# Splitting the modulation products of both first-block layers over three places of a one-core Trainium2 kernel

## The reference, cut to what matters

```python
def adaln(cond, w_mod, b_mod):
    return jnp.split(jax.nn.silu(cond) @ w_mod + b_mod, 6, axis=-1)      # w_mod: 1024 x 6144

for i in range(DEPTH):                                                   # 2 layers
    sh1, sc1, gt1, sh2, sc2, gt2 = adaln(c, w_mod[i], b_mod[i])
    csh1, csc1, cgt1, csh2, csc2, cgt2 = adaln(c_ctx[None, :], w_mod[i], b_mod[i])
    x, ctx = mixer_sublayer(x, ctx, (sh1, sc1, gt1), (csh1, csc1, cgt1), lp, rope, update_ctx)
    x = x + gt2[:, None, :] * peer_ffn(modulate(rmsnorm(x, g_norm2[i]), sh2, sc2), ...)
    if update_ctx:
        ctx = ctx + cgt2[:, None, :] * peer_ffn(modulate(rmsnorm(ctx, g_norm2[i]), csh2, csc2), ...)
```

## Time and profile before

| | us |
|---|---|
| median of 3 runs | 4714.18 (4707.75 to 4722.7) |
| profiled execution, time | 4724.5 |
| profiled execution, span | 4722.7 |
| mean granted TensorE clock | 0.867 of full |
| TensorE matmul busy | 3695.1 (78%) |
| VectorE busy | 2504.9 (53%) |
| moved by DMA | 1093.51 MB, 232 GB/s over the span |

### The profile page before, as it was taken

How to read it: one execution, slowest core, us unless ns; L and a number is a source line. 1 busy time by engine, 2 the same in 40 slices (tenths; PEclk the granted TensorE clock), 3 DMA queues, 4 the chain that set the end, 5 groups by cost and what they waited for, 6 DMA issues and landing times. The chain is left out here.

```text
span 4722.7 us, 46191 instructions
## 1 busy us (share of the span) xinstructions
PE 3695.1 (78%) x15562; PEld 2891.4 (61%) x15562; DVE 2504.9 (53%) x4840; ACT 627.5 (13%) x1654; POOL 1355.6 (29%) x1156
## 2 busy tenths in 40 slices
PE   5677989469988999967982444445999898998898
PEld 2345878458777777745771111113886787886787
DVE  0236557798788676654548878664433201333300
ACT  1223011230000000012210000101011201001200
POOL 0026000005665566623104777773000000000000
PEclk7787999699999999977896677767997799998799
DMA  9401844339999999950645999998861344771242
GB/s 338 155 13 40 243 123 119 103 117 406 409 409 377 409 409 409 409 196 30 181 154 218 386 372 363 390 394 299 277 209 45 107 134 143 243 245 50 90 151 98
DMA packets 549997, 1093.51 MB, mean 232 GB/s; under 512 B 29572, under 2 KB 315268, under 8 KB 549030
## 3 DMA queue, kind: packets, MB, share of 16 engines
q1 hardware_dynamic: 398216, 549.92, 34.0%
q0 software_dynamic: 147456, 536.94, 29.3%
q10 hardware_dynamic: 4128, 4.19, 0.3%
HBM read 1074.16 MB, written 16.78 MB: 231 GB/s over the span
## 5 line engine op out<-in xcount | busy, mean ns | idle before, releaser
L1897 PE MATMUL ps<-gv,diag 128*128 128x512 f32 x512 | 302.8, 757 | 402.3 <-DMA gv<-in_v_tab,eid 292.0
L1633 POOL DMA_INDIRECT gu<-in_u_tab,eid x256 | 346.2, 1353 | 837.4 <-DVE gate L1280 493.4
L2342 PE MATMUL ps<-hT,wring 128*128 128x256 f32 x2560 | 559.3, 379 | 0.2 <-DMA wring<-in_ffn_w_up 0.2
L1598 PE MATMUL ps<-hT,wring 128*128 128x256 f32 x2048 | 483.1, 390 | 76.9 <-DVE hT L1753 75.1
L2342 PEld LDWEIGHTS ps<-hT,wring 128*128 128x128 f32 x2560 | 486.2, 190 | 66.9 <-DVE hff L2409 0.6
L1598 PEld LDWEIGHTS ps<-hT,wring 128*128 128x128 f32 x2048 | 388.2, 193 | 166.3 <-DVE hT L1753 115.1
L1897 PEld LDWEIGHTS ps<-gv,diag 128*128 128x128 f32 x512 | 123.2, 248 | 580.2 <-issue 463.7
L1591 PE MATMUL ps<-hT,wring 128*128 128x256 f32 x2048 | 463.5, 379 | 1.4 <-ACT G L1674 1.4
L1591 PEld LDWEIGHTS ps<-hT,wring 128*128 128x128 f32 x2048 | 389.6, 190 | 54.5 <-issue 1.6
L2003 DVE CUSTOM_DVE_ANT_0 junk<-gu,htok 128x1024 f32<-128x1024 f32 x256 | 313.7, 1225 | 141.3 <-DMA gu<-in_u_tab,eid 133.3
L1777 DVE SCALAR_TENSOR_TENSOR wring<-gv,wgt,wring 128x1024 f32<-128x1024 f32 x254 | 326.4, 1285 | 112.2 <-DMA gv<-in_v_tab,eid 107.4
(11 more groups left out here) (317 smaller groups left out, 4721.3 us busy)
## 6 DMA issues: line engine op xcount, KB each, us to landing
wring<-in_u_first SPq DMA_DIRECT2D x128, 512.0 KB, 9.2
wring<-in_v_tab SPq DMA_DIRECT2D x128, 512.0 KB, 6.8
wring<-in_w_mod SPq DMA_DIRECT2D x24, 2048.0 KB, 12.9
lslot<-in_ada_w SPq DMA_DIRECT2D x32, 1536.0 KB, 10.5
wring<-in_ffn_w_gate SPq DMA_DIRECT2D x44, 1024.0 KB, 8.8
wring<-in_ffn_w_up SPq DMA_DIRECT2D x44, 1024.0 KB, 11.2
wring<-in_ffn_w_down SPq DMA_DIRECT2D x44, 1024.0 KB, 5.0
wring<-in_w_in SPq DMA_DIRECT2D x72, 512.0 KB, 6.6
```

The source lines that it names most:

```text
L1598: m = nc.tensor.matmul(ps[:, n // 2, (n % 2) * S:(n % 2 + 1) * S], vslot[:, e % 2, n * P:(n + 1) * P], act_[:, e % 3, :], start=e == 0 and ...
L1633: nc.gpsimd.indirect_dma_start(gu[:, n % RING, :], None, ub, bass.IndirectOffsetOnAxis(ap=eid[:, n // COLS, n % COLS:n % COLS + 1], axis=0 ...
L1897: m = nc.tensor.matmul(ps[:, mixed_banks(t) + b, :], diag[:, s, i, :], gv[:, BYDVE + i, b * 512:(b + 1) * 512], start=first, stop=last)
L2342: m = nc.tensor.matmul(ps[:, 4 + 2 * s + n, q * S:(q + 1) * S], up_slot(s, q)[:, k, n * P:(n + 1) * P], hT[:, k, 0:S], start=k == 0, stop= ...
```

## The change

The five opening phases become one, `opening`. It loads the conditions, four units of the first layer's modulation into four separate places (three in `wring`, one in `hT`), the identity and the table between them, then x, the context and the rope tables, and waits for all of these at its end. It computes units 0 to 3 (`sh1`, `sc1`).

The other eight units of the first layer are made in `queries`, as 16 half units of 256 columns with three slots in `wring`, between the Fourier branch and the transposes of the heads; their bias is added in `convolution_norm`. Six units of the second layer are made in the `scores_first` of x with two slots in the free `kT` and `qT`, and the other six as 12 half units in the build of `hybrid`, one at every second block from block 5 on. There the copies that VectorE made are ScalarE's. `load_u(0)` and `load_u(1)` move behind the build, since a slot of the half units lies in their place.

```diff
+    def opening(self, cols, weights, units, bias0):
...
             @block.sync
             def _(sp):
                 for b, name in enumerate(("cond_first", "cond_second")):
-                    sp.dma_start(raw[:, b], a[name]).then_inc(loaded.sem, 16)
+                    sp.dma_start(raw[:, b], a[name]).then_inc(condd.sem, 16)
+                sp.dma_start(slot(0), weights(0)).then_inc(w[0].sem, 16)
+                sp.dma_start(ident[:], a["ident"]).then_inc(turnd.sem, 16)
+                sp.dma_start(self.cols[:, 0:A_N], cols).then_inc(biasd.sem, 16)
+                for u in range(1, units):
+                    sp.dma_start(slot(u), weights(u)).then_inc(w[u].sem, 16)
+                sp.dma_start(xT[:, :, 0:S], a["xT"].rearrange("(k p) t -> p k t", p=P)).then_inc(loaded.sem, 16)
+                sp.dma_start(xT[:, :, S:2 * S], a["ctxT"].rearrange("(k p) t -> p k t", p=P)).then_inc(loaded.sem, 16)
+                for t, n in ((self.cosb, "rope_cos"), (self.sinb, "rope_sin")):
+                    sp.dma_start(t[:], a[n]).then_inc(loaded.sem, 16)
+                sp.wait_ge(loaded.sem, 64)
...
+    def queries(self, l, T, mods=None):
...
+                for i, hu in enumerate(half_units):
+                    if i >= 3:
+                        sp.wait_ge(rowed.sem, i - 2)
+                    sp.dma_start(half_slot(i), mods(hu, 256, 256)).then_inc(m_in[i % 3].sem, 16)
...
+                for i, hu in enumerate(half_units):
+                    if i == 0:
+                        pe.wait_ge(fcopied.sem, 2 * segs)
+                    pe.wait_ge(m_in[i % 3].sem, 16 * (i // 3 + 1))
+                    if i >= 2:
+                        pe.wait_ge(rowcopied.sem, i - 1)
+                    self.modulation_rows(half_slot(i), 256, i % 2).then_inc(rowed.sem, 1)
+                    if i:
+                        columns(pe, i - 1)
+                if half_units:
+                    columns(pe, len(half_units) - 1)
                 pe.wait_ge(fcopied2.sem, 2 * segs)
                 pe.wait_ge(dd.sem, after)
                 self.head_transposes(pe, None, qtok, tiles, qT, tfull, tcopied)
...
+    def scores_first(self, l, first_tile, weights, heads, ahead=None, mods=None):
...
+                for u in range(min(units, 2)):
+                    sp.dma_start(mslot[u % 2], mods(u)).then_inc(m_in[u % 2].sem, 16)
                 for h in range(H1):
                     sp.wait_ge(rest.sem, h + 1)
                     sp.dma_start(self.kept[first_tile + 1, :, h * 256:(h + 1) * 256], stage[:, h % 2, :]).then_inc(st[h % 2].sem, 16)
...
+                    if 2 <= h + 1 < units:
+                        sp.wait_ge(rowed.sem, h)
+                        sp.dma_start(mslot[(h + 1) % 2], mods(h + 1)).then_inc(m_in[(h + 1) % 2].sem, 16)
...
+                def modulate(u):
+                    pe.wait_ge(m_in[u % 2].sem, 16 * (u // 2 + 1))
+                    if u:
+                        columns(u - 1)
+                    self.modulation_rows(mslot[u % 2], 512, 6).then_inc(rowed.sem, 1)
+
+                def columns(u):
+                    pe.wait_ge(rowcopied.sem, u + 1)
+                    if u:
+                        pe.wait_ge(colcopied.sem, u)
+                    self.modulation_columns(modrow, 512, 7).then_inc(colturned.sem, 1)
...
                         score(h - 1)
+                    if 2 <= h < 2 + units:
+                        modulate(h - 2)
...
+                def copy_row(u):
+                    if u:
+                        act.wait_ge(colturned.sem, u)
+                        copy_columns(u - 1)
+                    act.wait_ge(rowed.sem, u + 1)
...
                         out(h - 1)
+                    if 3 <= h < 3 + units:
+                        copy_row(h - 3)
...
+    def hybrid(self, l, mods):
...
-                load_u(0)
-                load_u(1)
+                load_half(0)
+                load_half(1)
                 for b in range(NB):
                     sp.wait_ge(left.sem, 2 * b + 2)
                     sp.dma_start(late[:, :, b * FIRSTS * TB:(b + 1) * FIRSTS * TB].rearrange("q p n -> p q n"),
                                  leaving[:, b % 2].rearrange("p (q n) -> p q n", q=NQ)).then_inc(away[b % 2].sem, 16)
+                    i = unit_behind(b)
+                    if i is not None and i + 2 < HALF_UNITS:
+                        sp.wait_ge(rowed.sem, i + 1)
+                        load_half(i + 2)
+                sp.wait_ge(rowed.sem, HALF_UNITS)
+                load_u(0)
+                load_u(1)
                 for s in range(2):
                     sp.wait_ge(away[s].sem, 16 * NB // 2)
                 for e in range(NE):
...
+                        i = unit_behind(b)
+                        if i is not None:
+                            pe.wait_ge(m_in[i % 2].sem, 16 * (i // 2 + 1))
+                            if i:
+                                columns(i - 1)
+                            self.modulation_rows(mslot[i % 2], 256, i % 2).then_inc(rowed.sem, 1)
+                    columns(HALF_UNITS - 1)
...
                 def down(e):
+                    if e == 0:
+                        pe.wait_ge(colcopied.sem, HALF_UNITS)
```

More of the change, by code:

```diff
@@ L170, in memory, with slot @@
         self.wring = sb("wring", [P, 2, 6144])
[L173 to L193, removed]
+    def opening(self, cols, weights, units, bias0):
+        nc, a, ps, mod, xT, ident = self.nc, self.a, self.ps, self.mod, self.xT, self.ident
+        cond, raw, wide, both = self.cond, self.condraw, self.wide, self.both
+        first = len(self.held)
+        row = [self.sb("row", [P, 512]) for _ in range(2)]
+        flat = self.wring[:].rearrange("p s n -> p (s n)")
+        with self.phase("condd", "turnd", "biasd", "loaded", "w0", "w1", "w2", "w3", "act_done", "cleared", "summed", "rowed", "copied",
+                        "turned", "placed") as (
+                block, condd, turnd, biasd, loaded, w0, w1, w2, w3, act_done, cleared, summed, rowed, copied, turned, placed):
+            w = (w0, w1, w2, w3)
+            def slot(u):
+                return self.hT[:] if u == 3 else flat[:, u * KD * 512:(u + 1) * KD * 512].rearrange("p (k n) -> p k n", k=KD)
             @block.sync
@@ L1397, in scores_first @@
         at = first_tile * P
+        units = 6 if mods else 0
+        modraw = self.modraw
+        mslot = [b[:].rearrange("p h t -> p (h t)").rearrange("p (k n) -> p k n", k=KD) for b in (self.kT, self.qT)]
+        modrow = self.qtok[:].rearrange("p a b c -> p (a b c)")[:, 0:512]
         def slot(s):
             return self.wring[:, s, 0:KD * 512].rearrange("p (k n) -> p k n", k=KD)
-        with self.phase("loaded", "w1", "full", "copied", "sfull", "first", "rest", "dve_done", "stored0", "stored1", ahead=ahead) as (
-                block, loaded, w1, full, copied, sfull, first, rest, dd, st0, st1):
-            st = (st0, st1)
+        with self.phase("loaded", "w1", "full", "copied", "sfull", "first", "rest", "dve_done", "stored0", "stored1",
+                        "m0", "m1", "rowed", "rowcopied", "colturned", "colcopied", ahead=ahead) as (
+                block, loaded, w1, full, copied, sfull, first, rest, dd, st0, st1, m0, m1, rowed, rowcopied, colturned, colcopied):
+            st, m_in = (st0, st1), (m0, m1)
             @block.sync
@@ L2103, in first_layer @@
         load = self.merge_unit(l)[1]
-        self.convolution_norm(T // S, ahead=lambda sp, landed: load(sp, 0, 0, landed))
+        self.convolution_norm(T // S, l == 0, ahead=lambda sp, landed: load(sp, 0, 0, landed))
         mT = self.qT
```

217 lines of the change are left out of this document (126 added, 91 removed).

## The result

The changed kernel takes 4631.0 us (median of four runs, 4624.8 to 4635.6), the kernel before 4712.1 us: a ratio of 0.9824, 95% interval 0.9803 to 0.9844, and a gain of 81 us, with some 10 us of uncertainty to either side. The forecast was a gain of 99.5 us and 4615 us, the range 4598 to 4652. The direction and the range held; the size was 18 us too large.

A forecast was written before the change was run, and what follows sets the result against it. No single bound: weight loads bind the opening, VectorE the scores and build, DMA the main loop. Terms -127 + 16 + 6 + 1 + 4.5 = -99.5 us, from 4714.2 to 4614.7 us; range 4598 to 4652, its share under 4635 us given 70%.

The forecast's parts named there:

- Opening: Start of the kernel: unit 3 lands at 26.3 us, next phase begins at 33.3 us; gain 127 us, ends 124 and 129.
- Queries: Layer 1 queries: thirteen queued half loads, then transposes, end at 376.4 instead of 360.1 us; 16 us paid, ends 12 and 28.
- The cover by GpSimd: Queries: GpSimd and VectorE hide the first 14 us of the added work, and 16 us are paid.
- the flow: Queries: with loads always queued, halves of 1 MB follow one another every 2.86 us, at 367 GB/s.
- Scores of x: Second-layer units in the scores: 8.8 us a head at the higher clock; 6 us paid, ends 2 and 42.
- wrong if the clock falls in the scores or the build: Stated sign of a wrong prediction: the clock falls in either stage, or a late store holds ScalarE.
- the first rival, the lower clock in part: New places for the units: TensorE partly at the lower clock, 40 us more, 4655 us; range 4635 to 4690, chance 22%.
- The upper end of the stage, 42 us: Scores of x: 42 us paid if TensorE runs all of it at the lower clock, 14.6 us a head.
- Build: Gate build: VectorE's 3.53 us a block covers TensorE's added half units, clock no lower than 0.90; 1 us paid.
- Start of the loop: Main loop: u loads asked for after the build land like `v`, delaying `up(0)`; 4.5 us paid, between 2.6 and 7.
- Rival two, loads one by one: Queries: three slots fail to keep the queue full, 7.4 us a load, 57 us more, 4672 us; chance 4%.
- rival three, the loop at the lower clock: Main loop falls to the lower clock, 7 us more a step; at 20 steps 4755 us, slower than before; chance 3%.

The follow-up runs named there:

- sig_early: Changed kernel with ScalarE's two sigmoids right after the first root and the head norms' root behind the second row copy, in the queries; ratio 0.9806.
- row_first: Changed kernel with ScalarE copying a unit's modulation row at the head of a head's turn in the scores of x; 4620.5 us, ratio 0.9794.
- early_u: Changed kernel with the main loop's first two u loads issued in the gate build behind block 27's store; 4621.7 us, ratio 0.9807.
- Twelve: Changed kernel without GpSimd's share of the convolution taps in attend, both layers, part of the computation left out; attend of layer 1 took 79.6 us.
- early_rows: Changed kernel with the first three half units of the queries computed ahead of the Fourier branch; ratio 0.9804, queries 87.0 us.
- half_queries: Changed kernel with the last 8 of 16 half units in the queries left out, raw values zero-filled; queries took 69.6 us.
- before_again: The kernel before, unchanged, profiled a second time; queries 70.6 us, attend 87.1 us.
- combo: Changed kernel with row_first, early_u and early_rows together; 4640.3 us against 4755.8 for the kernel before on another chip, ratio 0.9751.

## Why the prediction was right, and where 18 us went

**Opening: right.** Unit 3 landed at 26.50 us (forecast 26.3), the last load at 32.86 (32.3). The gain over the profiled pair is 126.7 us (forecast 127). It is 124.7 over all profiles, because the second profile of before began `keys_values` 2.2 us earlier (its 24 issues took 120.7 instead of 121.9 us), 1.1 on the mean of the two, and because the norm runs 1.1 us longer behind the short opening (24.8 instead of 23.7).

**Queries: mechanism right, 3 us short.** The cover by GpSimd was priced well: with eight halves the stage costs nothing, with sixteen it pays for the flow. The forecast put the last landing at 241.9 us, counted from the new start of the stage (367.2 less 125.3); it came at 243.4. The mis-sized term is the flow, 3.01 us a half (348 GB/s) and not 2.86, which was taken from a single microsecond of x's landing; over twelve halves it is 1.8 us. Two of the twelve landings lie 3.65 and 4.14 us behind the one before, another 1.8 us, and half 3 landed 2.0 us sooner than forecast, at 205.55. The three slots are not what holds the flow back: the first three halves, asked for together, land 3.00 and 2.92 us apart too. Why they flow more slowly than x, in runs of the same size, is open. The 2.8 us that the forecast gave TensorE for a half at the lower clock is the 2.81 of the rows. The rest is the tail: 11.4 us from the last product to the first attention product, forecast 10.2 with the barrier. TensorE's wait for ScalarE's table loads was not foreseen, and sig_early shows that it cost about 1 us, because the flow takes its place.

**Scores of x: the step that failed is the choice of the clock.** By its own sign ("wrong if the clock falls in the scores or the build") the forecast was wrong here. It took 8.8 us a head "since TensorE will be busy for 7.2 of 8.8 us". The first full head does take 8.72, at clock 1.00. Then the first rival, the lower clock in part, sets in: three heads of 10.39 us are 4.8 us over the forecast's three, and score 2 started 0.6 us late (763.90, forecast 867.4 less 104.1). That is 5.4 of the 6 us missing. That the time still lies under 4635 us, in the share given to the forecast and not to this rival, is luck of its size: only three heads ran at 10.39 us. The upper end of the stage, 42 us, was too high by the forecast's own steps, too: score 2 at 862.2 + 3.64 + 6.6 = 872.4 and four heads of 14.6 us give 34. I had the wait for ScalarE in the sum as time, and not as what lets the clock fall. The experiment row_first takes away the wait and with it both. What it leaves open is why the first head with the same wait (1.33 us) still ran at clock 1.00. The Trainium skill, "TensorE: Matmul & The Clock Gate" (A second HAM failure mode: psum-queue depth-cycling), describes short idles of TensorE between groups of matmuls that make the clock swing; these heads agree with it, at an idle of 1.36 us and a clock of 0.84.

**Build: right.** 3.53 us a block, clock 0.90 as before, nothing paid.

**Start of the loop: mechanism right, 3 us short.** The term "4.5 us, as `v`" is 5.7 us for two loads issued together; the idle of 6.79 us then adds 1.5 us to the first two products (8.65 us instead of 7.15). That the loop carries it in full was right: early_u brings back 6 us.

**Attend: missing from the sum.** The forecast costed only the one added operation in `convolution_norm`. `attend` is untouched and still took 2.9 us more on the mean of four profiles. That most of this depends on how VectorE's and GpSimd's taps fall together is shown (Twelve). Why they fell worse in these four than in the two of before is open, and so is whether they did: `attend` moves by 5 us between profiles of the same code, and the kernels with early_rows or sig_early and nine early taps took 86.1 to 87.0 us again, half_queries 92.9. Over all nine the excess is 1.5 us. That it goes with how the phase is entered is a guess.

The terms missed add up: 2.3 (opening), 3.2 (queries), 2.9 (attend), 5.9 (scores) and 2.8 (loop), less 1.5 in the build, are 16 of the 18 us; the remaining 2 are well within the measurement. Nearly all of them point the same way, so the range held by its width and not because errors cancelled. Rival two, loads one by one, and rival three, the loop at the lower clock, did not occur: 3.0 us a half, and a window of the loop at 409 GB/s as before.

## What to carry to other kernels

Loads moved out of a bound stretch were free in a stage up to the cover that another engine gives (eight of sixteen halves here), and from there on cost nearly their flow (2.5 us each); count the cover first, then the slots that keep the flow going. Work that is added to TensorE between short waits should be priced at the lower clock too: here an order of the copies that removes a wait of 1.4 us gave back 9.8 us over six units. Whatever a bound loop needs first must be asked for ahead of the last work before it.

## What the runs showed of the hardware

**VectorE and GpSimd.** A tap of VectorE on 128 x 512 numbers takes 0.75 us alone and up to 1.87 beside GpSimd's operations, which themselves take from 1.26 to 2.15 us. The Trainium skill, "SBUF — State Buffer" (SBUF: two separate sides), calls this an exclusive lock on a shared pair of ports for a VectorE operation with two inputs in SBUF, held for a whole instruction; the sizes fit, 0.75 plus most of one GpSimd operation.

**Issuing.** SyncE's issue of a load takes some 0.4 us, but 2.9 to 7.5 us when several megabytes are outstanding (in the opening, from the third unit to the first rope table, which is small). What stands behind it in SyncE's queue is issued later by so much: the last rope table at 26.71 us. Here it cost nothing that shows, since the loads landed one behind another all the same (29.52, 32.30, 32.50, 32.86 us).

**Spread.** In an unchanged stage of layer 2 the profiles differ by 31 us: 356 to 367 on the chip of before_again, early_rows, combo and half_queries, 336 to 349 elsewhere. In `attend` they differ by 5.4 us (3.2 on one chip), in `project` of layer 2 by 0.02. A single pair of traces can't carry a claim of a few microseconds in the first two, and a pair from two chips not even one of ten.
